# A hybrid decoder layer in fp32 on one core: the recurrence moved to the operand buffers, and elementwise work moved between VectorE, ScalarE and GpSimd

## What is computed

```
mod = silu(c) @ w_ada + b_ada                     # shift, scale, gate, twice
h = rms_norm(x) * (1 + scale_m) + shift_m
u = h @ w_in + b_in                               # value | glu gate | recurrent | gelu gate
ya = silu(layer_norm(conv31(value * sigmoid(glu)))) 
hb = rg_lru(conv4(recurrent)); yb = hb * gelu(gelu_gate)
x = x + gate_m * (concat[ya, yb] @ w_out)
x = x + gate_f * (relu(h2 @ w_up)^2 @ w_down);  y = rms_norm(x)
# rg_lru: a = exp(-8 sigmoid(ga) softplus(-lambda)), h_t = a h_(t-1) + sqrt(1 - a^2) sigmoid(gx) x_t
```

## Time and profile before

| | |
|---|---|
| median of 3 runs | 1300.93 us (1299.98 to 1302.32) |
| the profiled execution's own time | 1299.89 us |
| its span, first to last instruction | 1298.1 us |
| mean granted clock of TensorE in it | 0.962 |
| TensorE matmul busy | 1197.8 us, 92% of the span |
| VectorE, ScalarE, GpSimd busy | 737.4, 406.2, 348.1 us |

### The profile page before, as it was taken

How to read it: one execution, slowest core, us unless ns; L and a number is a source line. 1 busy time by engine, 2 the same in 40 slices (tenths; PEclk the granted TensorE clock), 3 DMA queues, 4 the chain that set the end, 5 groups by cost and what they waited for, 6 DMA issues and landing times.

```text
span 1298.1 us, 16535 instructions
## 1 busy us (share of the span) xinstructions
PE 1197.8 (92%) x6175; PEld 1065.9 (82%) x6175; DVE 737.4 (57%) x840; ACT 406.2 (31%) x707; POOL 348.1 (27%) x201
## 2 busy tenths in 40 slices
PE   6687999999555999899999999999999999999996
PEld 2586999998324888888998998998998988988985
DVE  1658699998598445534434534534535435435457
ACT  2743543352935333430320320320410310311322
POOL 0237788453042010320320410410410311311300
PEclk9796999999877999999999999999999999999998
DMA  9424333422012500210220210210300300301102
GB/s 298 161 65 130 98 97 107 134 82 66 0 51 69 167 33 1 73 57 1 66 65 1 81 48 0 82 48 0 97 32 0 97 32 5 92 32 32 49 33 105
DMA packets 74661, 87.25 MB, mean 67 GB/s; under 512 B 3816, under 2 KB 53248, under 8 KB 74627
## 3 DMA queue, kind: packets, MB, share of 16 engines
q1 hardware_dynamic: 72448, 85.21, 21.0%
q10 hardware_dynamic: 2179, 1.61, 0.5%
HBM read 81.72 MB, written 5.08 MB: 67 GB/s over the span
## 4 chain that ended last, share of the span: by engine, by line
PE 81%; DVE 8%; ACT 4%; SPq 2%; issue 2%; DMA 1%; POOL 1%; ACTq 0%; DVEq 0%; POOLq 0%
PE ps L1455 14%; PE ps L1457 14%; PE ps L1456 14%; PE ps L1596 11%; PE ps L1597 11%; PE ps L1599 11%; PE ps L1603 1%; PE ps L1602 1%; SPq L257 1%; PE ps L1348 1%; PE ps L1347 1%; DVE rec L1196 1%; DMA x<-in_x_prompt 1%; SPq L263 1%; ACT aw_hi L563 1%
## 5 line engine op out<-in xcount | busy, mean ns | idle before, releaser
L1455 PE MATMUL ps<-act_hi,w_hi 128*128 128x384 f32 (+1 forms) x1152 | 378.7, 329 | 4.5 <-DVE act_lo L1009 3.9
L1457 PE MATMUL ps<-act_hi,w_lo 128*128 128x384 f32 (+1 forms) x1152 | 377.0, 327 | 0.0
L1456 PE MATMUL ps<-act_lo,w_hi 128*128 128x384 f32 (+1 forms) x1152 | 376.8, 327 | 0.0
L1455 PEld LDWEIGHTS ps<-act_hi,w_hi 128*128 128x128 f32 x1152 | 217.4, 189 | 7.0 <-ACT act_hi L536 4.0
L1456 PEld LDWEIGHTS ps<-act_lo,w_hi 128*128 128x128 f32 x1152 | 217.4, 189 | 1.7
L1255 DVE TENSOR_TENSOR ps<-ps,gt_p 128x1024 f32<-128x1024 f32 x72 | 88.7, 1233 | 228.9 <-PE ps L1599 228.9
L1457 PEld LDWEIGHTS ps<-act_hi,w_lo 128*128 128x128 f32 x1152 | 217.2, 189 | 0.0
L357 POOL TENSOR_TENSOR w_lo<-raw,w_hi 128x1024 fp32r<-128x1024 f32 x48 | 118.2, 2464 | 356.8 <-ACT w_hi L541 295.8
L357 POOL TENSOR_TENSOR wb_lo<-raw,wb_hi 128x1024 fp32r<-128x1024 f32 x36 | 91.7, 2557 | 433.5 <-ACT wb_hi L541 424.8
L1596 PE MATMUL ps<-wb_hi 128*128 128x512 f32 x512 | 199.4, 389 | 1.1 <-ACT gt_s L867 1.1
L1597 PE MATMUL ps<-wb_lo,wb_hi 128*128 128x512 f32 x512 | 199.2, 389 | 0.0
(11 more groups left out here) (227 smaller groups left out, 1314.3 us busy)
## 6 DMA issues: line engine op xcount, KB each, us to landing
raw_ada<-in_w_ada SPq DMA_DIRECT2D x32, 512.0 KB, 3.7
raw<-in_w_up SPq DMA_DIRECT2D x32, 512.0 KB, 4.0
raw<-in_w_down SPq DMA_DIRECT2D x32, 512.0 KB, 3.3
ada<-in_w_ada SPq DMA_DIRECT2D x8, 1024.0 KB, 15.0
x<-in_x_prompt SPq DMA_DIRECT2D x16, 512.0 KB, 8.9
raw<-in_w_in SPq DMA_DIRECT2D x16, 512.0 KB, 5.2
raw<-in_w_out SPq DMA_DIRECT2D x8, 512.0 KB, 3.3
out<-x SPq DMA_DIRECT2D x8, 512.0 KB, 2.6
```

Source lines behind the costliest of these rows:

```text
L1455: mm(out, wh, xh, start=(k == 0), stop=False)
L1456: mm(out, wh, xl, start=False, stop=False)
L1457: last = mm(out, wl, xh, start=False, stop=(k == KD - 1))
```

## The change

It has several parts:

- **Buffers.** The decays, gates, their squares and the squares of the layer norm move from `lru`, `rec`, `sg` and `sq` to `tmp_a`, `tmp_b`, which lie over `act_hi`, `act_lo`. Each tile has its own place, so waits between tiles (`q_done` ahead of the second gate) go. `w_out` pieces 0 to 3 can be split before the recurrence ends; pieces 4 to 6 wait for `h_done` 1, 2, 3. `LO_SLOT` orders the low parts in `wb_lo`.
- **Early in the projections.** GpSimd splits adaLN pieces 0 and 1 ahead of `product(0)`. TensorE takes pieces 2 and 3 of group 0 behind the first chunk of step 1. The small softplus terms of lambda move from the convolutions to the start.
- **Means.** They stand behind chunks 1 and 2 of the last step's first strip and chunk 0 of its second one; `centre` stands between the group B convolutions on VectorE.
- **Normalisation.** The squares and variances stand ahead of the recurrence. Reciprocal and scaling run between the gates' operations. Gain, shift and swish become one `Silu` on ScalarE with scale and bias, four operations per chunk; the Sigmoid, the gain-and-shift operations and VectorE's product are gone.
- **Recurrence.** Two of the three Tanh of a gate are one. The square of the decay, the product with the gelu branch and the end-state copies are on GpSimd. The end state is turned behind the second output tile and stored from `h_st`.
- **Output weights.** Low parts: GpSimd pieces 0, 1, 2, 3, 4, 6, VectorE 5 and 7.

```diff
+        rs = shared([("h_st", [9, WA], F32)], [("w_hi", [P, 2, D], F32R)])
...
+                    [("tmp_a", [P, KD, TOK], F32), ("tmp_b", [P, KD, TOK], F32)],
...
-        a_t = [lru[:, j, :] for j in range(J)]
-        m_t = [rec[:, j, 0:TOK] for j in range(J)]
+        a_t = [tmp_b[:, J + j, :] for j in range(J)]
+        m_t = [tmp_a[:, J + j, :] for j in range(J)]
+        a2_t = [tmp_b[:, j, :] for j in range(J)]
+        gx_t = [tmp_a[:, j, :] for j in range(J)]
+        xsq = tmp_b[:, 0:J, :]
+        LO_SLOT = (2, 3, 4, 7, 5, 6, 0, 1)
...
-            product(0)
             split_ada(0, 0)
             split_ada(1, 1)
+            product(0)
...
+            pool.wait_ge(convb_tap, 2 * KB * J)
+            pool.wait_ge(var_done, NC)
+            for j in range(J):
+                w_out_lo(j)
+                pool.wait_ge(a_done, j + 1)
+                pool.tensor_tensor(a2_t[j], a_t[j], a_t[j], ALU.mult).then_inc(a2_done, 1)
+                if j == 2:
...
+                    last.then_inc(tails, 1)
...
+            for j in range(J):
+                pool.wait_ge(h_done, j + 1)
+                pool.tensor_tensor(gel[:, j, :], m_t[j], gel[:, j, :], ALU.mult).then_inc(yb_done, 1)
+                pool.tensor_copy(h_end[:, j, 0:1], m_t[j][:, SEQ - 1:SEQ])
...
+                if j == 1 or j == 3:
+                    w_out_lo(J + j - 1)
```

ScalarE's new order behind the projections, and its new operations:

```diff
+            squares(0)
+            squares(1)
+            squares(2)
+            act.wait_ge(ada_lo, 4 * 2 * J)
+            w_out_hi(0)
+            for c in range(NC):
+                deviation(c)
+            w_out_hi(1)
+            staged(0, stage[0:KA - 1, 2, :], 6, KA - 1)
...
+            staged_a(0)
+            recurrence(0)
+            staged_a(1)
+            staged(3, stage[64:64 + KB - 1, 2, :], 7, KB - 1)
...
+            recurrence(1)
+            w_out_hi(2)
+            staged(4, stage[32:32 + NB * (KB - 1), 2, :], 6, NB * (KB - 1))
...
+            recurrence(2)
+            w_out_hi(3)
+            recurrence(3)
...
+                for i in range(J):
+                    last = act.activation(conv_a[:, i, t0:t0 + w], conv_a[:, i, t0:t0 + w], ACT.Silu,
+                                          scale=par[:, C_LNG + i:C_LNG + i + 1], bias=par[:, C_LNB + i:C_LNB + i + 1])
...
+            ya(0)
+            act.wait_ge(h_done, 1)
             w_out_hi(4)
+            yb_hi(0)
+            ya(1)
+            act.wait_ge(h_done, 2)
             w_out_hi(5)
+            yb_hi(1)
+            ya(2)
+            act.wait_ge(h_done, 3)
             w_out_hi(6)
+            yb_hi(2)
             w_out_hi(7)
+            yb_hi(3)
```

VectorE and TensorE:

```diff
+            normalise(0)
+            normalise(1)
+            gated_input(0)
+            normalise(2)
+            for j in range(1, J):
+                gated_input(j)
...
+            dve.wait_ge(q_done, J)
+            dve.wait_ge(a2_done, J)
...
             ya_lo(0)
+            yb_lo(0)
             w_out_lo(5)
+            ya_lo(1)
+            yb_lo(1)
+            ya_lo(2)
+            yb_lo(2)
             w_out_lo(7)
+            yb_lo(3)
...
-                        if last and s == 1:
-                            mean_a(c)
+                        if last and 1 <= 3 * s + c <= NC:
+                            mean_a(3 * s + c - 1)
...
-                for i in range(4):
-                    ada_piece(0, i)
+                ada_piece(0, 0)
+                ada_piece(0, 1)
...
+            step(1, late=(2, 3))
```

More of the change, by code:

```diff
@@ L587, in _ @@
             norm_x(0)
+            act.wait_ge(par_cp, 1)
+            own(act.activation(sp[:, 0, :], par[:, C_LAM:C_LAM + J], ACT.Abs))
+            act.activation(sp[:, 1, :], sp[:, 0, :], ACT.Exp, scale=-1.0).then_inc(k_done, 1)
+            act.wait_ge(k_done, 2)
+            act.activation(sp[:, 3, :], sp[:, 2, :], ACT.Ln).then_inc(k_done, 1)
             norm_x(1)
@@ L784, in _ @@
                 act.activation(m_t[j], m_t[j], ACT.Tanh, scale=k4[:, 0, j:j + 1], bias=k4[:, 0, j:j + 1]).then_inc(th_done, 1)
[L785 to L792, removed]
+                gate_act(gx_t[j], 3, gate_x, j, 1, evac_b)
             def staged(n, dst, bank, r):
@@ L869, in _ @@
             gates_out(0, 4, 6)
[L870 removed]
+            act.wait_ge(staged_out, 16 * 5)
             act.wait_ge(sc_done, 2)
@@ L1473, in var_a, with step @@
                 pe.wait_ge(sq_done, c + 1)
-                wait(pe, sd_done, c)
-                mean(c, 7, lambda j: sq[:, j, 0:CW[c]], var_done)
-            def step(m, last=False):
+                if c == 1:
+                    pe.wait_ge(ada_evac, ADA_G)
+                if c == 2:
+                    pe.wait_ge(sd_done, 1)
+                mean(c, 6 + c % 2, lambda j: xsq[:, j, c * CH:c * CH + CW[c]], var_done)
+            def step(m, last=False, late=()):
                 for s, done in ((0, strip_a), (1, strip_b)):
@@ L1486, in step @@
                         if c == 0 and s == 0:
+                            for i in late:
+                                ada_piece(m - 1, i)
                             group_turn(m + ADA0 - 1, 7, 0)
@@ L1530, in _, with turn_state, recurrent_gates @@
             pe.wait_ge(xc_done, NC)
-            for j in range(J):
+            def turn_state(n, bank, r, src):
+                wait(pe, st_cp, n - 1)
+                for j in range(J):
+                    last = nc.tensor.transpose(ps[0:r, bank, j * P:(j + 1) * P], src(j), ident[:, :])
+                last.then_inc(st_tr, 1)
+            def recurrent_gates(j):
                 pe.wait_ge(convb_tap, 2 * KB * (j + 1))
@@ L1624, in _ @@
                         pe.wait_ge(gt_cp, 2)
+                        pe.wait_ge(hend_done, J)
+                        for j in range(J):
+                            last = nc.tensor.transpose(ps[0:9, 4, j * P:(j + 1) * P], h_end[:, j, :], ident[:, :])
+                        last.then_inc(st_tr, 1)
+                    if t == 2:
+                        pe.wait_ge(st_cp, 6)
                     turn(t - 1, t - 1, xn[:, 0, :])
```

289 lines of the change are left out of this document (121 added, 168 removed).

## The result

The changed kernel takes 1297.36 us (1296.29 to 1298.74, 9 runs) against 1300.93 for the kernel before (1298.97 to 1303.02, 9 runs, on the same chip). The ratio is 0.9974, with a 95% interval from 0.9964 to 0.9985: 3.6 us faster, where I had forecast no change (1301.2, range 1288 to 1309). The profiled span is 1295.4 us against 1298.1, at a granted clock of 0.960 against 0.962.

What follows compares the result with a forecast made beforehand. Bound: the chain from TensorE's projections through VectorE's recurrence and normalisation to the first output tile. Projections end 319.9, last gate 360.5, scans 368.9 to 395.0, tile done 425.6: net plus 0.3, forecast 1301.2 us, range 1288 to 1309.

Steps and rivals of the forecast that it cites:

- Early start: At the start: two GpSimd splits ahead of the first product; first turn 112.1 instead of 120.03, minus 6.0 us net.
- The softplus terms: At the start: moving lambda's logarithm terms there costs nothing, and freeing VectorE before its last convolutions gains nothing.
- Means: In the projections: the same matmuls, only the last turn now exposed; plus 0.9 us.
- Projections' end: End of the projections on TensorE at 319.9 us, against 325.0 before.
- ScalarE to the last gate: From the projections' end to the last gate: ScalarE's work sums to 40.6 us, last gate out at 360.5.
- GpSimd's queue: In the gates: GpSimd and VectorE take turns; VectorE's last operation ends at 368.9, and only then the scan loop starts.
- Scans: In the scan loop: 17.8 us for four tiles plus 8.3 for held port, a split and end copies, ending at 395.0.
- Tail 17.2, tile 13.4: After the scans: 17.2 us to the first output tile, then 10.9 plus 2.5 for a lower-clock start, done at 425.6.
- (a): In the gates: GpSimd's queue is not late, VectorE's last gate operation ends at 361.8, 7 earlier; 1292 us; chance 0.28.
- (b): Gates and scans: no exclusion between GpSimd and VectorE; scans from 363, tile done near 405; 1280 us; chance 0.04.
- (c): Gates and scans: GpSimd becomes the bound, scan loop starts at 373; 6 us slower in all, 1307; chance 0.28.
- (d): Whole kernel: moved work and new waiting cancel, 1296 to 1307 us; chance 0.40, the likeliest.

Runs made afterwards that it cites:

- e2: The kernel before with the early start alone (first product behind two adaLN splits, pieces 2 and 3 behind the first strip); ratio 0.9964 to the kernel before.
- e1: The changed kernel with the early start undone (first product ahead of the adaLN splits, all four pieces before the first turn); ratio 0.9999 to the kernel before.
- e5: The changed kernel with 25 unread matmuls of 128 columns behind the two late pieces, before the first turn; ratio 0.9946 to the kernel before.
- e7: The kernel before with only the softplus of lambda moved to the start; ratio 0.9964 to the kernel before.
- e12: The changed kernel with 12 unread matmuls of 128 columns between the last turn and the variances; ratio 0.9951 to the kernel before.
- e4: The changed kernel with GpSimd's sixteen gt_tok copies moved behind the last square; ratio 0.9952 to the kernel before.
- e10: The kernel e8 with three added unread two-input GpSimd products of 1024 columns, released by scans 1 to 3; ratio 0.9963 to the kernel before.
- e13: The kernel before with both early parts, the early start and the softplus moved to the start, and nothing else; ratio 0.9932 to the kernel before.
- e8: The changed kernel with gelu products, end copies and splits of pieces 4 to 6 on VectorE, gt_tok copies behind the last square; ratio 0.9905 to the kernel before.
- e11: The kernel e8 with three added unread one-input GpSimd copies of 1024 columns, released by scans 1 to 3; ratio 0.9929 to the kernel before.
- e3: The changed kernel with the gelu products and end-state copies back on VectorE behind the scans; ratio 0.9946 to the kernel before.

## Why the prediction was wrong

The time lies in the range, but the forecast of no change was wrong: it was a difference of large terms, and those at the start were mis-sized. Point by point:

- **Early start, "minus 6.0".** Wrong size: alone it moved the last turn by 3.3 (e2), in the changed kernel by 3.9 (e1). I had the first turn 7.9 earlier; it came 5.9 earlier in e2, where the loads stand in front of it, and 6.9 in the changed kernel against e1 (111.53 against 118.38). And I gave 1.8 back for a restart of some 4 us, reading a stretch of plain strips in the earlier trace rows (the counts of those rows would give 1.3, the starts of the matmuls, 0.32 us apart against 0.17, give 1.8). It took 2.6 (e2) to 3.0: the turn too runs at 0.50 (plus 0.8), and TensorE stays there for 6 us, from 111.53 to about 117.6. e5 shows that this is the clock. The end of the fourth adaLN split was right (105.1 forecast, 105.45 measured); from there the forecast's terms add up to 111.7, not 112.1.
- **The softplus terms, "nothing".** This is the step that failed: a term put at nothing that was worth 3.3 us. I priced what the moved operations cost at their new place and never what they had cost at the old one. I even counted "the loop's table load (1.28)" into the new turn at 112.1, in the belief that it belonged to the loop; it belonged to the Exp ahead of it. Removed were the Exp and two loads ahead of the first turn and a hold of 0.7 us in each of three steps: 3.3 at the last turn (e7). At the new place there are three loads (20.44, 21.96 and 25.07 us), not two, and what follows is 0.3 (e1) to 0.8 (e7) later, not nothing.
- **Means, plus 0.9.** Right: the last step of e1 (288.62 to 320.96) takes 32.3 against 31.5 before, 0.8 more.
- **Projections' end.** 318.1 measured, 319.9 forecast. These 1.8 us, carried on to the end of the first tile, are most of the error of 2.9 us (2.6 faster in the rows, plus 0.3 forecast). The early start gave 2.1 less than forecast (3.9 for 6.0), and the softplus, put at nothing, gave 3.3 (e7) to 3.9 (e1, with the 0.8 of the means added back), so the two misses partly cancel.
- **ScalarE to the last gate, 40.6 us.** Measured 42.8 (318.14 to 360.95). I had 1.75 us of waiting for the third variance; at granted clock 0.50 the variances held the last root until 330.80 (328.60 in e12). The extra drain of 1.38 us per table switch, which the Trainium skill, "ScalarE: Activation LUTs", section "What ACT_TABLE_LOAD costs", adds, is again not in the rows: the load at 334.25 ends at 335.53 and its Tanh starts at 335.54.
- **GpSimd's queue, last operation at 368.9.** Measured 366.7. Right in kind: the chain runs through split 2, square 2, the copies, split 3 and square 3 as written. The copies took 5.0 where I took 3.0, but nothing was added by turns, as VectorE's operation at 360.98 simply lost (4.52) instead of getting in between.
- **Scans, 26.1 us.** Measured 25.8. Each product held VectorE by 2.1, three times, and the split of piece 4 by 2.1, where I had 2.3.
- **Tail 17.2, tile 13.4.** Measured 16.8 and 13.8; the turn of end states as forecast.
- **Rivals.** (a) needed GpSimd's queue not to be late; it was, and e4 shows the price of its copies, about 2 us at the gating and not 7. (b) is refuted by e10. (c) decided at square 3 ending after 370; it ended at 364.3. (d), the forecast, had the right mechanism from 318 on: from the last turn to the gating the changed kernel needs 106.1 us, the kernel before 100.5, so 5.6 more where I had forecast 6.2. That this sum came out so near is in part luck: ScalarE's chain was 2.2 longer and GpSimd's queue not taken by turns.
- **The signs.** The first turn (111.53), the last Tanh (ends at 360.95) and the stretched operations among the scans are as written; the last turn (317.08) and the first tile (409.32) are 2 and 3 us earlier than written.

Put together: the two early parts, less the means, gave 6.9 at the projections' end, where I had 5.1; the rest took back 5.6 at the first tile and had 1.2 returned in the second, where I had 6.2 and 0.9. What the change does besides its two early parts costs some 5 us (e1 against e7, 0.9999 and 0.9964; the changed kernel against e13, 0.9974 and 0.9932), of which 0.8 are the means. Most of it comes through the work given to GpSimd: with that taken back (e8) the same change stands at 0.9905, below e13. How much of the rest of e8's gain is due to Silu, to the moved variances or to the earlier output weights was not taken apart.

## What to carry to other kernels

When an operation is moved, price what it did to its old neighbours: on ScalarE look for the table loads behind it, above all ahead of a loop, where one foreign function can put two loads into every pass. Before giving a GpSimd operation work from the end of a VectorE chain, ask whether VectorE goes on with two-input operations just then: a product of some 1000 columns takes 1.28 on VectorE and costs it 2.1 from GpSimd. And a hole in TensorE can cost twice, once as idle time and once as a restart at the lower level. It did so at three places here, two of which the change had opened or moved, and a few unread matmuls removed the second cost.

## What the runs showed of the hardware that I had not expected

- One Exp ahead of a loop of Sigmoid and Copy, and the Ln behind it, cost eight table loads, six of them in the three passes of the loop. With both gone, e1 shows none on ScalarE between 82 and 261 us; three loads at 20 to 27 us are new.
- A one-input copy of 1024 columns on GpSimd takes 1.04 us and held a two-input operation of VectorE by 0.85 (e11); a two-input product takes 2.35 and held it by 2.17 (e10). A square with the same tensor on both inputs takes 2.00 for 1088 columns, a product of two tensors 2.48 (345.31 and 371.34 in the changed kernel).
- Sixteen GpSimd copies of 64 columns got through in VectorE's gaps in 11.7 us in e4 and cost none of its operations more than 0.07, while one split of 1024 columns beside the same kind of work lasted 7.66 in e3.
- In the changed kernel TensorE ran at granted clock 1.00 up to the last turn, was idle for 2.35 us behind it, and the variances ran at 0.50 from 320 to 326. In e12, with 12 matmuls in that stretch, the clock stayed at 1.00.
